# Two transformer blocks on one core: both token tiles' mixers of the first layer ahead of the first expert gather

## What is computed

```python
cond = silu(c)                                     # one vector of 1024
for l in range(2):
    sh1, sc1, g1, sh2, sc2, g2 = split(cond @ w_ada[l] + b_ada[l], 6)
    h = rms_norm(x) * (1 + sc1) + sh1
    proj = h @ w_in[l]                             # 1024 x 1280: pool part, q, k, v
    y = [multiscale_pool(proj), window_attention(q, k, v, sinks)]
    x = x + g1 * (rms_norm(y) @ w_out[l])          # 1024 x 1024      (the "mixer" ends here)
    h2 = rms_norm(x) * (1 + sc2) + sh2
    q = h2 @ peer_wq[l]                            # 8 heads: each lists 16 of 16384 experts per token
    # a = gelu(h2 . u[e]) * gate, for the 128 listed experts e of each token
    x = x + g2 * sum_e a[e] * v[e]
```

## Time and profile before

| what | value |
|---|---|
| median of 3 runs | 2364.1 us (2360.09 to 2368.74) |
| the profiled execution | 2370.28 us |
| its span | 2368.5 us |
| PE, DVE, ACT, POOL busy | 89%, 52%, 35%, 25% of the span |
| moved by DMA | 767.01 MB, mean 324 GB/s |
| last chain, by engine | PE 58%, DMA 25%, DVE 9%, ACT 5% |
| mean granted clock of PE | 0.963 |

### The profile page before, as it was taken

One profiled execution on the slowest core, in us unless ns is written; L12 is line 12 of the kernel. 1 busy time (PEld: TensorE's weight loads), 2 busy tenths in 40 slices (PEclk: granted clock), 3 DMA queues, 4 the chain that ended last, 5 costly groups with the idle time before them and its releaser, 6 DMA issues.

```text
span 2368.5 us, 24191 instructions
## 1 busy us (share of the span) xinstructions
PE 2117.9 (89%) x8236; PEld 1251.3 (53%) x8236; DVE 1229.6 (52%) x2911; ACT 822.9 (35%) x2348; POOL 602.3 (25%) x564
## 2 busy tenths in 40 slices
PE   6779989888989888989987888889999999999998
PEld 4535545434545434645433333437856667766665
DVE  2327777776767676776876667754520002441001
ACT  1214554444554344554443444533310001331000
POOL 1123333444334343433444434420000000000000
PEclk9889999999999899999999999999899999999999
DMA  9999999999999999999999999983343432342420
GB/s 381 417 395 427 426 427 427 427 427 420 426 427 411 426 427 417 426 422 426 424 427 405 427 427 427 416 369 110 154 157 149 171 131 76 108 194 109 171 102 18
DMA packets 107711, 767.01 MB, mean 324 GB/s; under 512 B 12210, under 2 KB 12482, under 8 KB 15939
## 3 DMA queue, kind: packets, MB, share of 16 engines
q0 software_dynamic: 80640, 587.24, 59.1%
q1 hardware_dynamic: 26948, 178.23, 19.1%
HBM read 764.38 MB, written 1.05 MB: 323 GB/s over the span
## 4 chain that ended last, share of the span: by engine, by line
PE 58%; DMA 25%; DVE 9%; ACT 5%; issue 2%; POOL 0%; DVEq 0%; ACTq 0%; POOLq 0%
PE PS L513 56%; DMA BIG<-in_uv,EID 22%; DVE BIG L1620 3%; DMA BIG<-in_wada 3%; ACT DG L966 1%; DMA MOD<-in_uv,EID 1%; ACT L1149 1%; DVE BIG L1313 1%; DVE SC L1389 1%; PE PS L625 1%; PE PS L592 1%; ACT AV L966 1%; ACT BIG L1035 0%; DVE X L1303 0%; DVE BIG L1299 0%
## 5 line engine op out<-in xcount | busy, mean ns | idle before, releaser
L513 PE MATMUL PS<-BIG,DG 128*128 128x512 f32 x1820 | 888.8, 625 | 159.7 <-ACT DG L966 141.2
L1620 DVE CUSTOM_DVE_ANT_0 BIG<-BIG,H 128x1024 f32<-128x1024 f32 x455 | 558.1, 1227 | 357.7 <-DMA BIG<-in_uv,EID 327.8
L454 POOL DMA_INDIRECT BIG<-in_uv,EID x455 | 510.1, 1121 | 766.7 <-PE PS L513 744.1
L513 PEld LDWEIGHTS PS<-BIG,DG 128*128 128x128 f32 x1820 | 332.3, 195 | 611.2 <-issue 297.2
L513 PEld LDWEIGHTS PS<-HT,BIG 128*128 128x128 f32 x2304 | 350.3, 193 | 76.4 <-issue 47.8
L513 PE MATMUL PS<-HT,BIG 128*128 128x128 f32 (+1 forms) x2304 | 383.6, 323 | 7.3 <-DVE HT L1299 3.5
L1149 ACT ACTIVATE AV<-AV 128x1 f32<-128x1 f32 x512 | 103.2, 201 | 666.9 <-DVE AV L1620 662.9
L513 PE MATMUL PS<-BIG,HT 128*128 128x256 f32 (+3 forms) x1216 | 299.7, 404 | 10.6 <-DVE HT L1299 3.6
L513 PE MATMUL PS<-BIG 128*128 128x512 f32 (+7 forms) x792 | 282.4, 528 | 1.8 <-DVE BIG L1299 1.8
L513 PEld LDWEIGHTS PS<-BIG,HT 128*128 128x128 f32 x1216 | 230.9, 196 | 80.0 <-issue 48.8
L1303 DVE TENSOR_TENSOR BIG<-BIG 128x256 f32<-128x256 f32 (+1 forms) x96 | 49.4, 515 | 383.5 <-ACT BIG L1284 381.3
(11 more groups left out here) (173 smaller groups left out, 1271.4 us busy)
## 6 DMA issues: line engine op xcount, KB each, us to landing
BIG<-in_wada POOLq DMA_DIRECT2D x43, 1024.0 KB
BIG<-in_win SPq DMA_DIRECT2D x36, 1024.0 KB, 6.0
BIG<-in_wup SPq DMA_DIRECT2D x32, 1024.0 KB, 6.9
BIG<-in_wdn SPq DMA_DIRECT2D x32, 1024.0 KB, 4.8
BIG<-in_wq SPq DMA_DIRECT2D x28, 1024.0 KB
BIG<-in_wout SPq DMA_DIRECT2D x24, 1024.0 KB, 5.4
BIG<-in_uv,EID POOLq DMA_INDIRECT x455
MOD<-in_wada POOLq DMA_DIRECT2D x5, 1024.0 KB
```

The source lines that it names most:

```text
L454: pool.e.indirect_dma_start(out=slot(u), out_offset=None, in_=I[f"uv{l}"], in_offset=bass.IndirectOffsetOnAxis(ap=EID[:, t * 128 + j:t * 1 ...
L513: return pe.e.matmul(dst, a, b, start=start, stop=stop)
L1620: v.e.tensor_tensor_reduce(out=JD, in0=slot(u)[:, 0:1024], in1=H[:, t, :], scale=1.0, scalar=0.0, op0=ALU.mult, op1=ALU.add, accum_out=AV[ ...
```

## The change

In `drive`, both mixers of layer 0 are advanced in one loop of 102 steps, tile 1's eleven steps behind tile 0's (`apart=11`). Heads 0 and 1 of tile 0 start at steps 79 and 89 of it, and `early` is advanced nine times at step 4, once at each of thirteen steps from 18 to 56, and at every step above 71. No mixer is started beside the gathers of tile 0 any more.

`behind` puts tile 1's last two output blocks, and all that follows them, twelve steps later. SP loads the `win` and `wout` blocks of layer 0 once, and a slot is free when tile 1 has used it. As tile 1's steps stand eleven behind, the five `win` blocks stay in the four slots longer: the fifth is issued when tile 1's first projection (step 18) is done, and tile 0 uses it at step 19. The rows of layer 1's modulation wait for tile 1's scores, whose banks they use, and PE's single banks are four (4 to 7) until the first head takes bank 7. The diff, without empty lines and with the repeated edits of one kind cut:

```diff
-            n2=71, T2=74, end=78, sk=6, top=10, head=22, enter=88, rows=6)
+            n2=71, T2=74, end=78, sk=6, top=10, head=22, enter=88, rows=6, apart=11)
+def behind(l, t, j):
+    return 12 if (l, t) == (0, 1) and j > 1 else 0
...
-                    load(in_w, ("win", l, t, j), I["win1"][l * 5 + j], 2048, ("pe.proj", l, t, j))
+                    if (l, t) != (0, 1):
+                        load(in_w, ("win", l, t, j), I["win1"][l * 5 + j], 2048, ("pe.proj", l, t if l > 0 else 1, j))
...
-                    yield from k.to(WHEN["out"] + 2 * j)
-                    load(in_w, ("wout", l, t, j), I["wout1"][l * 4 + j], 2048, ("pe.out", l, t, j))
+                    yield from k.to(WHEN["out"] + 2 * j + behind(l, t, j))
+                    if (l, t) != (0, 1):
+                        load(in_w, ("wout", l, t, j), I["wout1"][l * 4 + j], 2048, ("pe.out", l, t if l > 0 else 1, j))
...
         def drive(pre, head, early, late, experts, finish, enter):
-            mixer = pre(0, 0)
-            for k in range(WHEN["T0"] + 1):
-                next(mixer)
-            for _ in range(9):
-                next(early, None)
-            for k in range(WHEN["T0"] + 1, WHEN["end"] + 1):
-                next(mixer, None)
-                if k in range(18, 57, 3) or WHEN["n2"] <= k < WHEN["n2"] + 3:
+            mixers, h0, h1 = (pre(0, 0), pre(0, 1)), head(0, 0, 0), head(0, 0, 1)
+            for k in range(WHEN["end"] + WHEN["head"] + 2):
+                for _ in range(9 if k == WHEN["T0"] + 1 else 1 if k in (18, 21, 26, 29, 32, 37, 40, 43, 46, 48, 50, 53, 56) or k > WHEN["n2"] else 0):
                     next(early, None)
-            h0, h1 = head(0, 0, 0), head(0, 0, 1)
-            for k in range(WHEN["head"] + 1):
-                next(h0, None)
-                if k >= 10:
+                next(mixers[0], None)
+                if k >= WHEN["apart"]:
+                    next(mixers[1], None)
+                if k > WHEN["end"]:
+                    next(h0, None)
+                if k > WHEN["end"] + 10:
                     next(h1, None)
-                if k >= 8:
-                    next(early, None)
             for _ in early:
                 pass
...
-                        if b == (4 if p == 1 else 2):
+                        if p > 0 and b == (4 if p == 1 else 2):
                             live.append(pre(*TILES[p + 1]))
...
                 if b == 0:
                     pe.wait_ge(*at("v.zc"))
-                    pe.wait_ge(*at("v.bias", "m", 0, 0, 1))
+                    pe.wait_ge(*at("v.bias", "m", 0, 1, 1))
...
+            singles.places = [4, 5, 6, 7]
...
-                    w = have(in_w, ("win", l, t, j))
+                    w = have(in_w, ("win", l, t if l > 0 else 0, j))
...
                 if (l, t) == (0, 1):
-                    pe.wait_ge(*at("v.cols", 1))
+                    pe.wait_ge(*at("v.bias", "m", 0, 0, 1))
...
-                    yield from k.to(WHEN["out"] + 2 * j)
+                    yield from k.to(WHEN["out"] + 2 * j + behind(l, t, j))
                     have_hT(l, t, 1)
-                    w = have(in_w, ("wout", l, t, j))
+                    w = have(in_w, ("wout", l, t if l > 0 else 0, j))
...
-                yield from k.to(WHEN["T2"])
+                yield from k.to(WHEN["T2"] + behind(l, t, 3))
                 transposes(l, t, 2, ("v.h2", l, t))
...
                 if n > 0:
                     pe.wait_ge(*at("a.s", *TILES[(n - 1) // 8], (n - 1) % 8))
+                else:
+                    singles.places = [4, 5, 6]
+                    pe.wait_ge(*at(*singles.held[7]))
```

More of the change, by code:

```diff
@@ L1116, in pre @@
                 evac_hT(l, t, 1)
-                yield from k.to(WHEN["n2"])
+                yield from k.to(WHEN["n2"] + behind(l, t, 3))
                 a.wait_ge(*at("v.out", l, t, 3))
                 rms_in_hT(f"n2{t}", ("n2", l, t), t, [X[:, t, :]], 1024.0)
-                yield from k.to(WHEN["T2"] + 2)
+                yield from k.to(WHEN["T2"] + 2 + behind(l, t, 3))
                 evac_hT(l, t, 2)
@@ L1532, in pre @@
                 for j in range(4):
-                    yield from k.to(WHEN["out"] + 2 * j + 3)
+                    yield from k.to(WHEN["out"] + 2 * j + 3 + behind(l, t, j))
                     v.wait_ge(*at("pe.out", l, t, j))
@@ L1540, in pre @@
                     stt(sc2, sc2, 1.0, par1("n2"), ALU.add, ALU.mult).then_inc(*up("v.c"))
-                yield from k.to(WHEN["n2"] + 2)
+                yield from k.to(WHEN["n2"] + 2 + behind(l, t, 3))
                 s = inverse(f"n2{t}", 1, ("n2", l, t))
@@ L1545, in pre @@
                 tt(H[:, t, :], H[:, t, :], sh2, ALU.add).then_inc(*up("v.h2", l, t))
-                yield from k.to(WHEN["T2"] + 3)
+                yield from k.to(WHEN["T2"] + 3 + behind(l, t, 3))
                 evac_hT(l, t, 2)
```

## The result

The changed kernel takes 2400.2 us (2397.0 to 2402.2, four runs), the kernel before 2364.5 in the same session: a ratio of 1.015, 95% interval 1.0127 to 1.0173. It is 36 us slower. The profiled executions, 2398.7 and 2370.3 us, are 28.4 us apart; that of before took longer than each of its four timed runs, so I compare traces with the 28 and times with the 36. The forecast had the side right and the size wrong (+11, upper bound +23).

What follows compares the result with a forecast made beforehand. Until the last gather lands, time is bytes over DMA rate (427 GB/s). Lost transfer time ahead of the gathers, +33.4 us, and saved bytes, -22.1, gave +11.3: 2375 us against the 2364.1 median, range 2361 to 2387.

Steps and rivals of the forecast that it cites:

- the -22.1 us for nine blocks: Tile 1's five input and four output blocks no longer loaded: 9.44 MB at 427 GB/s, -22.1 us.
- the move of the mixer out of the gather stretch for nothing: Tile 1's mixer leaves the first gathers' stretch; PE gains about 50 us, but DMA covers it, so 0.
- the starving of the DMAs between steps 57 and 71: No modulation slots freed there; DMAs idle after 103.9 us until tile 1's first output block ends: 45.5 us lost.
- R: End on PE of tile 1's first output block, which frees the first query block's slot: 149.4 us, forecast 145 to 157.
- the way from R to the list: PE's work after R, then the first gather's list, ready at 196 us, 10 us early, so costing nothing.
- R - 138.1: The whole change in one line: lost transfer time ahead of the gathers less saved bytes, +11.3 us at R 149.4.
- The wait for the shared fifth block: PE before tile 0's fifth projection: 6.0 us for its load, bounds 2.5 and about 12; block then cold, 5.9.
- Late operands: PE waits on exponentials, copies and adds from ScalarE and VectorE before R: 6.5 us, bounds 0 and 12.
- The list is late: Rival: first gather's list at 216 us instead of 196, ten us added, +21, 2385 us; chance 0.09.
- one of my own signs of being wrong: At the first gather: the prediction counted as wrong if that gather waits for its list.
- Faster: Rival: saved bytes outweigh DMA starving; R below 131 gives over 0.3% faster, 2357 or 2342 us; chance 0.13.
- the same: Rival: PE's walk loses nothing to waits, R 137, sum -1, 2363 us, within 0.3%; chance 0.25.

Runs made afterwards that it cites:

- e4: The kernel before, with tile 1's nine weight blocks not loaded (its result is wrong): 2347.5 us, ratio 0.9916.
- e1: The changed kernel with tile 1 loading its own nine `win` and `wout` blocks again instead of sharing tile 0's: 2382.0 us, ratio 1.0062.
- e3: The changed kernel with four early steps put before tile 0's fifth projection, in the wait for the shared block: 2382.2 us, ratio 1.0078.
- e11: The changed kernel with the early steps of 53 and 56 moved to 51 and 52: 2390.8 us, ratio 1.0112.
- e2: The changed kernel with one early step also at each step from 58 to 71: 2399.4 us, ratio 1.0141.
- e8: The changed kernel with four early steps at step 19 and one each at 59, 62, 65 and 68: 2382.0 us, ratio 1.0077.

## Why the prediction was wrong in size

**What held.** The bound (bytes over rate until the last gather), the -22.1 us for nine blocks (e4: -19.0 in the last product), the move of the mixer out of the gather stretch for nothing (the account needs no term for it), the starving of the DMAs between steps 57 and 71, and the way from R to the list (46.6 us forecast, 211.96 - 165.70 = 46.3 measured). The line of the sum, R - 138.1, gives +27.6 with the measured R; the profiled executions are 28.4 apart.

**The step that failed is R**, the walk along PE's order: 165.7 instead of 149.4, even above my upper bound of 161. Part by part:

- The wait for the shared fifth block: taken as 6.0 us, a median of issue to landing; it was 9.3. PE reached it 1.3 us sooner than forecast (55.6 instead of 56.9), so the fifth block started at 64.96 instead of 62.9: +2.1. My upper bound of 12 held. e1 and e3, without this wait and its cold block, end 15 and 13 us sooner; these are not prices of the wait alone, as e1 has more and e3 earlier loads to fill the DMAs with.
- Late operands behind it: 10.0 us (1.48, 0.47, 0.47, 3.62, 1.71 and 2.28) instead of 6.5: +3.5. The places were those named: ACT's norm with its table load ahead of tile 1's copy of P, and DVE's work for tile 0 ahead of its copy before tile 1's first output block. There it was not so much the adds, which end at 158.06 as PE's transposes do, as a product for tile 0's second norm behind them (158.17, 1.22 us); the copy ends at 160.2, PE goes on at 160.29.
- The largest, +10.7, is what is left of the 16.3, and it is a term that I had set to zero. From the end of the fifth block (70.75) to R PE was not waiting for 84.9 us, where I had 74.1. I had costed all this work at full clock. PE's granted clock was 0.69 in the window of 110 to 120 us and 0.50 from 130 to 140; the second half of tile 1's scores took 3.55 us (1.99 in e11), its first values 3.67 where 1.9 was taken, its first two output blocks 8.83 instead of 6.9. Taking for each slow piece its time at full clock elsewhere in the traces (3.45 us for a block, 1.54 for an early step), I estimate the lower clock's share at 12 us, and the work itself 2 us shorter than I had summed. I had let the clock fall once, in the fifth block, though I named five more places for waits. e1 repeats the slow pieces behind the same waits; e11, whose walk was 9.9 us shorter with 1.4 us less of waits, got the rest from faster matmuls.

The Trainium skill ("TensorE: Matmul & The Clock Gate", "HAM oscillation — how this bites in real kernels") says that a kernel whose bursts of matmuls are parted by waits for DMA pays the cold clock again after each wait. The block behind the 9.3 us wait for DMA agrees with it (5.86 us instead of 3.6). So do the transposes behind 3.6 us (1.97 us instead of 1.1), though that wait was for ACT. The scores do not come under it: that half of them took 3.55 us behind a wait of 0.47. A forecast by this rule of the Trainium skill would have priced a cold start for every wait on the list.

**The rivals.** "The list is late" was not what made it slower. The first gather did wait 6.0 us for it, one of my own signs of being wrong, but blocks were still in the queue, and the DMAs ran at 426 and 427 GB/s from 205 to 225 us; the sign should have been idle DMAs, not a waiting POOL. e2 and e8 showed how near it was. "Faster" needed R below 131, "the same" R between 131 and 145. The bound of some 358 GB/s per core for loads from HBM that the Trainium skill gives ("DMA: Bandwidth & Descriptors", "Where 436 GB/s comes from") was exceeded in the gather stretch of every kernel here, which runs on one core (423 or 424 GB/s from 240 to 1500 us, 427 in many slices); the Trainium skill itself, on the same page under "Measured (HBM→SBUF, 128 partitions, SWDGE, issued from GpSimd)", ties the figure to both cores of an HBM domain streaming.

**The rest of the 36 us.** 28.4 are in the traces; the medians lie further apart because the profiled execution of before took 5.8 us longer than its median, and that of the changed kernel 1.5 us less. Across sessions the median of before was 2363.2 to 2367.5 us.

## What to carry to other kernels

Where a kernel is bound by transfers, work moved ahead of the bound stretch costs its full time there if it stands between the transfers' issuer and what frees its buffers; count how many buffers that order frees, and when, before counting the bytes saved. A shared load that must stay in a small ring becomes a just-in-time load for its last block: put other work (here the very steps that free the other ring) into that wait. Price the walk along an engine with the clock that follows each wait, not at full speed with waits added.

## What the runs showed that I had not expected

- A weight block of 1.05 MB, for which the page gave 6.0 us from issue to landing as the median, took 9.3 us (issued at 55.67, used at 64.96), with POOL's blocks of 40 to 53 us partly still to be moved, and PE's wait for it was 9.3, 9.4, 9.5 and 9.7 us in the four kernels that put nothing into it.
- PE's clock was at different levels at the same place of the same order of instructions: in the changed kernel the granted clock of 110 to 120 us was 0.69 and the second half of tile 1's scores took 3.55 us, in e11, equal up to there, 1.00 and 1.99 us; in e1 they took 2.33 and in e3 3.73. In the changed kernel and e11 PE had been busy over 9 of the 10 us before, with short matmuls. What decides between the two levels there stays open.
